# A hybrid encoder layer: both heads of a pair side by side on the array, gates and branches with stationary weights, one schedule for all heads

## What is computed

```python
h = rmsnorm(x, norm_mix)
proj = h @ w_in      # rq, rk (4 x 128), rv, rg (4 x 256), aq, ak, av (24 x 64), gates (2 x 1024)
# retention, 4 heads: q, k rotated; scores (T x T) times a decay that falls with distance both ways
ret = rms(((q @ k.T) * decay) @ v) * ret_norm
branch_a = (silu(rg) * ret) @ w_ret_out
# attention: 8 heads, each in 3 groups (window 128, dilation 1; 512, 4; 2048, 16), one softmax over
# the keys of all three
branch_b = (num / den) @ w_att_out
merged = sigmoid(gate0) * branch_a + sigmoid(gate1) * branch_b
x = x + merged @ w_out
x = x + expert_choice_ffn(rmsnorm(x, norm_ffn))   # 16 SwiGLU experts, 64 tokens of each group per expert
y = rmsnorm(x, norm_final)
```

## Time and profile before

| what | us |
|---|---|
| median of 3 runs | 2798.7 |
| profiled execution | 2800.46 |
| its span, first to last instruction | 2798.6 |
| PE busy | 2628.1 (94%) |
| DVE busy | 1607.9 (57%) |
| ACT busy | 1379.5 (49%) |
| POOL busy | 407.3 (15%) |
| mean granted TensorE clock | 0.971 |

### The profile page before, as it was taken

One profiled execution on the slowest core, in us unless ns is written; L12 is line 12 of the kernel. 1 busy time (PEld: TensorE's weight loads), 2 busy tenths in 40 slices (PEclk: granted clock), 3 DMA queues, 4 the chain that ended last, 5 costly groups with the idle time before them and its releaser, 6 DMA issues.

```text
span 2798.6 us, 42036 instructions
## 1 busy us (share of the span) xinstructions
PE 2628.1 (94%) x15186; PEld 2298.4 (82%) x15186; DVE 1607.9 (57%) x1945; ACT 1379.5 (49%) x1544; POOL 407.3 (15%) x341
## 2 busy tenths in 40 slices
PE   7999999999969999999999939999999999999995
PEld 7988888889869888888889838888888888888884
DVE  2443434432342443434432358888888888888885
ACT  4332323332243333333432227777777777777774
POOL 4121212111013212121111030000000000000000
PEclk9999999999989999999999969999999999999997
DMA  4111111112232111111122269999999999999995
GB/s 169 46 69 47 68 47 68 51 56 98 106 144 84 54 61 57 58 58 58 37 84 91 92 254 351 383 385 385 388 380 392 379 390 380 392 377 395 377 376 191
DMA packets 130053, 551.19 MB, mean 197 GB/s; under 512 B 9089, under 2 KB 9217, under 8 KB 119665
## 3 DMA queue, kind: packets, MB, share of 16 engines
q1 hardware_dynamic: 122592, 522.81, 49.0%
q0 software_dynamic: 7312, 26.39, 3.2%
HBM read 528.20 MB, written 20.97 MB: 196 GB/s over the span
## 4 chain that ended last, share of the span: by engine, by line
PE 75%; issue 17%; POOL 3%; DVE 2%; ACT 2%; DMA 1%; POOLq 0%; DVEq 0%; SPq 0%; ACTq 0%
PE bank L908 37%; PE bank L692 27%; PE bank L707 3%; PE bank L744 2%; POOL rot L539 2%; PE bank L937 2%; PE bank L771 1%; PE bank L749 1%; ACT w_hi L1001 1%; POOL w_lo L550 1%; PE bank L775 1%; PE bank L872 1%; PE bank L797 0%; DVE h_lo L1514 0%; DVE y_tile L1771 0%
## 5 line engine op out<-in xcount | busy, mean ns | idle before, releaser
L1693 DVE TENSOR_TENSOR m_lo<-m_raw,m_hi 128x2048 fp32r<-128x2048 f32 x381 | 869.9, 2291 | 123.7 <-ACT m_hi L1243 121.8
L1243 ACT ACTIVATE m_hi<-m_raw 128x2048 fp32r<-128x2048 f32 x384 | 737.3, 1921 | 266.8 <-PE bank L908 266.8
L692 PE MATMUL bank<-w_hi,h_hi 128*128 128x256 f32 (+1 forms) x2304 | 717.4, 311 | 23.1 <-issue 15.3
L692 PE MATMUL bank<-w_lo,h_hi 128*128 128x256 f32 (+1 forms) x2304 | 698.3, 303 | 0.0
L692 PE MATMUL bank<-w_hi,h_lo 128*128 128x256 f32 (+1 forms) x2304 | 698.2, 303 | 0.0
L692 PEld LDWEIGHTS bank<-w_hi,h_hi 128*128 128x128 f32 x2304 | 445.7, 193 | 35.7 <-issue 28.2
L692 PEld LDWEIGHTS bank<-w_lo,h_hi 128*128 128x128 f32 x2304 | 446.7, 194 | 0.0
L692 PEld LDWEIGHTS bank<-w_hi,h_lo 128*128 128x128 f32 x2304 | 445.7, 193 | 0.0
L908 PE MATMUL bank<-m_hi,xs_hi 128*128 128x512 f32 x1040 | 324.2, 393 | 1.4 <-DVE xs_lo L1715 1.4
L908 PE MATMUL bank<-m_hi,xs_lo 128*128 128x512 f32 x1040 | 321.2, 390 | 0.0
L908 PE MATMUL bank<-m_lo,xs_hi 128*128 128x512 f32 x1040 | 321.2, 390 | 0.0
(11 more groups left out here) (175 smaller groups left out, 3077.6 us busy)
## 6 DMA issues: line engine op xcount, KB each, us to landing
m_raw<-in_w_exp_gate SPq DMA_DIRECT2D x128, 1024.0 KB, 7.7
m_raw<-in_w_exp_up SPq DMA_DIRECT2D x128, 1024.0 KB, 7.7
m_raw<-in_w_exp_down SPq DMA_DIRECT2D x128, 1024.0 KB, 7.5
w_raw<-in_w_b SPq DMA_DIRECT2D x24, 1536.0 KB, 6.4
w_raw<-in_w_a SPq DMA_DIRECT2D x24, 1024.0 KB, 4.8
w_raw<-in_w_c SPq DMA_DIRECT2D x24, 1024.0 KB, 4.8
xt<-in_x SPq DMA_DIRECT2D x16, 512.0 KB, 6.5
w_raw<-in_w_d SPq DMA_DIRECT2D x8, 1024.0 KB, 4.8
```

The lines of the kernel that those rows point to most:

```text
L692: last = pe.matmul(ps_proj[:, proj.slot, 0:cols], a[:, c, tokens], v[:, c, :], start=c == n == 0, stop=c == chunks - 1 and n == 2)
L1243: act.activation(m_hi[slot.slot][:, :, :], m_raw[raw.slot][:, :, :], ACT.Copy)\
L1693: dve.tensor_tensor(m_lo[slot.slot][:, :, :], m_raw[raw.slot][:, :, :], m_hi[slot.slot][:, :, :].bitcast(F32), ALU.subtract)\
```

## The change

1. **Pairs.** S is split: `S r` makes the 512-column scores of both heads (a = 0, 1) for residue r, `D r` the 128-column ones, one head after the other in each group; `T r` transposes four blocks of each head, `U r` the two small ones of both; one `V` makes both heads' outputs, alternating between the heads. `prob_t` holds both heads. Each head of a pair has its bank of `ps_sc` and of `ps_out`, and PE waits for both banks.
2. **Order.** The attention units of pair 0 come first, alone. Then three times: retention head h with the scores of pair h, then the units of pair h+1, with T3, U3 and V of pair h and the *whole* retention of head h. The last head's T3, U3, V and retention lie in the first column. G comes after V. The last `R` of the attention units comes after the first tile of the next head, so no transposes end the loop's body. As the next pair's v is projected before V has read the old one, it goes to `v_next` and is copied. SP loads in the new order. The first unit is now 384 columns wide (POOL's first split 3072 elements instead of 2048).
3. **Columns.** `project_turned` takes 128 weight columns as the stationary operand and moves 512 tokens. The outputs are features by tokens, so they are what w_out needs and `merged`'s transposes go: ACT rounds the sum to `mixed_hi`, DVE takes `mixed_lo`, and w_out's first tile waits chunk by chunk (`s_mixed`). The units' order is gate 0, gate 1, branch b, branch a.
4. **Reload.** x for the residual goes to `xr`, in the place of `h_hi`, after the last gates and behind the first w_out unit; `gain_ffn` beside it. So the experts' `m_hi` slots are reversed, and ACT's second split waits until x is stored.

```diff
--- before.py
+++ after.py
...
+def head_schedule():
+    order = "P S0 P D0 P P T0 S1 P U0 D1 P P T1 S2 P U1 D2 P P T2 S3 P U2 D3 P"
+    tiles = [(u, i) for u in range(3) for i in range(NT)]
+    out, behind = [], [("R", NG - 1, NT - 1)]
+    for word in order.split():
+        if word != "P":
+            out.append((word[0], int(word[1])))
+            continue
+        u, i = tiles.pop(0)
+        out.append(("P", u, i))
+        if i < len(PIECES):
+            out.append(("W", i))
+        if behind:
+            out.append(behind.pop(0))
+        if u == 0:
+            behind.append(("R", None, i))
+    assert not tiles and not behind
+    return out
...
+def attention_schedule(tail):
+    extra = {0: (("T", 3),), 1: (("U", 3),), 2: (("V",), ("G",)), 3: (("K", 0), ("K", 1)),
+             4: (("K", 2), ("K", 3)), 5: (("O", 0), ("O", 1)), 6: (("O", 2), ("O", 3)),
+             9: (("A", 0),), 10: (("A", 1),)} if tail else {}
     out, behind = [], []
     for n in range(NG * NT):
         g, i = divmod(n, NT)
         out.append(("P", g, i))
         if i < len(PIECES):
             out.append(("W", i))
+        out.extend(extra.get(n, ()))
         if behind:
             out.append(behind.pop(0))
         behind.append(("R", g, i))
+    return out
+COLUMN_UNITS = (0, 1, 3, 2)
+FIRST_COLUMN = {(0, 0): (("T", 3),), (0, 1): (("U", 3), ("V",), ("G",)), (1, 0): (("K", 0), ("K", 1)),
+                (1, 1): (("K", 2), ("K", 3)), (3, 0): (("O", 0), ("O", 1), ("O", 2), ("O", 3)),
+                (3, 1): (("A", 0), ("A", 1))}
+def column_schedule(first):
+    out = []
+    for u in COLUMN_UNITS:
+        for cc in range(COLS):
+            out.append(("C", u, cc))
+            if first:
+                out.extend(FIRST_COLUMN.get((u, cc), ()))
     return out
...
+        def all_read(eng, frees, t, but=0):
+            done = Tally(2)
+            done.items, done.laps, done.k = t.items, t.laps, t.k - but
+            eng.wait_ge(frees[0], START + done.lap + done.slot)
+            eng.wait_ge(frees[1], START + done.lap)
...
+                    if n == 0:
+                        sp.wait_ge(s_proj, START + b * PER_BATCH["proj"] + GATES_DONE)
                         apart(sp, s_apart_sp)
                         for i in range(NT):
...
+            def project_turned(chunks, hi, lo, cc, ready=None):
+                sl = w.slot
+                wh = w_hi[sl][:, 0:chunks * NC].rearrange("p (c n) -> p c n", c=chunks)
+                wl = w_lo[sl][:, 0:chunks * NC].rearrange("p (c n) -> p c n", c=chunks)
+                pe.wait_ge(s_proj_free[proj.slot], START + proj.lap)
+                for c in range(chunks):
+                    if ready is not None and c in ready:
+                        pe.wait_ge(s_lo, ready[c])
+                    for n, (v, a) in enumerate(((wh, hi), (wl, hi), (wh, lo))):
+                        last = pe.matmul(ps_proj[:, proj.slot, :], v[:, c, natural(cc)], a[:, c, :],
...
+                elif what == "S":
+                    r = arg[0]
+                    if r == 0:
+                        all_read(pe, s_tr_free, tr, but=1)
+                    all_read(pe, s_sc_free, sc)
+                    for a in range(2):
+                        pe.matmul(ps_sc[:, a, :], qk_t[0][head_rows(a), 0, natural(r)], qk_t[0][head_rows(a), 1, :],
+                                  start=True, stop=True).then_inc(s_sc, 1)
+                        sc.k += 1
+                elif what == "D":
+                    r = arg[0]
+                    if r == 0:
+                        all_read(pe, s_tr_free, tr)
+                    all_read(pe, s_sc_free, sc)
+                    for g in (1, 2):
+                        for a in range(2):
+                            last = pe.matmul(ps_sc[:, a, P * (g - 1):P * g], qk_t[g][head_rows(a), 0, natural(r)],
+                                             qk_t[g][head_rows(a), 1, natural(r)], start=True, stop=True)
+                            if g == 2:
+                                last.then_inc(s_sc, 1)
+                                sc.k += 1
+                elif what == "T":
+                    for a in range(2):
+                        pe.wait_ge(s_prob, step.n(1))
+                        transposes([prob[a][:, natural(j)] for j in range(4)])
+                        step.k += 1
+                elif what == "U":
+                    transposes([prob[a][:, natural(j)] for a in range(2) for j in (4, 5)])
+                elif what == "V":
+                    all_read(pe, s_tr_free, tr)
+                    all_read(pe, s_out_free, outs)
+                    for r in range(RES):
+                        for a in range(2):
+                            pe.matmul(ps_out[head_rows(a), a, :], v_a[0][:, r, head_rows(a)], prob_t[:, a, r, :],
+                                      start=r == 0, stop=False)
+                    for g in (1, 2):
+                        for r in range(RES):
+                            for a in range(2):
+                                last = pe.matmul(ps_out[head_rows(a), a, natural(r)], v_a[g][:, r, head_rows(a)],
+                                                 prob_t[:, a, RES + g - 1, natural(r)],
+                                                 start=False, stop=g == 2 and r == RES - 1)
+                                if g == 2 and r == RES - 1:
+                                    last.then_inc(s_out, 1)
+                                    outs.k += 1
...
+                def column(first):
+                    los = START + b * PER_BATCH["lo"]
+                    for what, *arg in column_schedule(first):
+                        if what in "TUV":
+                            attention_step(what, arg)
+                        elif what in "KOA":
+                            retention_step(what, arg)
...
+                        elif what == "C":
+                            u, cc = arg
+                            if cc == 0:
+                                unit_ready()
+                            if u < 2:
+                                project_turned(KC, h_hi, h_lo, cc)
+                            elif u == 3:
+                                project_turned(HP, a_hi, a_lo, cc, {0: los + HP} if first else None)
                             else:
...
-                pe.wait_ge(s_merged, START + b * PER_BATCH["mix"] + 16)
-                for i in range(NT):
-                    for half in range(2):
...
+                                project_turned(KC, r_hi, r_lo, cc,
+                                               {0: los + HP + 6, 6: los + HP + 7, 7: los + HP + 8} if first else None)
+                            if cc == COLS - 1:
+                                w.k += 1
+                column(True)
+                with rolled(pe, D // NC - 1, t, PER_COL):
+                    column(False)
                 for n in range(D // NC):
                     unit_ready()
                     for i in range(NT):
-                        project(NC, KC, h_hi, h_lo, natural(i))
+                        project(NC, KC, mixed_hi, mixed_lo, natural(i),
+                                b * PER_BATCH["mix"] if n == i == 0 else None)
...
+                    outs.k += 2
+                    if tail:
+                        all_read(act, s_proj_free, proj)
+                        act.wait_ge(s_out, START + outs.n())
+                        act.activation(v_a[0][:, 0:NT - 1, :], v_next[:, :, :], ACT.Copy)
...
+                def mixed_his(first):
+                    for cc in range(COLS):
+                        act.wait_ge(s_merged, START + t["mix"].n(1))
+                        operand_hi(mixed_hi[:, bass.ds(first + cc, 1), :], gates[:, 0, cc:cc + 1, :])
+                        t["mix"].k += 1
...
+                    elif unit.k == 1:
+                        act.wait_ge(s_n2, START + NB * NT)
+                        act.wait_ge(s_store_x, 16 * NB * NT)
...
+                elif what == "D":
+                    dve.wait_ge(s_tr, tr.n())
+                    for a in range(2):
+                        dve.wait_ge(s_sc, sc.n(1))
+                        apart(dve, s_apart_dve)
+                        dve.tensor_tensor_reduce(
+                            out=prob[a][:, T:T + 2 * P], in0=ps_sc[:, sc.slot, 0:2 * P],
+                            in1=mask12[:, :], scale=1.0, scalar=-3.0e38,
+                            op0=ALU.add, op1=ALU.max, accum_out=top[:, 2 * a + 1:2 * a + 2])\
+                            .then_inc(s_sc_free[sc.slot], 1)
+                        sc.k += 1
+                        all_read(dve, s_sc_free, sc)
+                        dve.tensor_scalar(shift[:, a:a + 1], top[:, 2 * a:2 * a + 1], top[:, 2 * a + 1:2 * a + 2],
+                                          -DH ** -0.5, ALU.max, ALU.mult).then_inc(s_sm, 1)
+                        score.k += 1
+                    for a in range(2):
+                        scale_step(a)
+                elif what == "T":
...
```

(89 more changed lines are left out.)

798 lines of the change are left out of this document (341 added, 457 removed).

## The result

| | before | after |
|---|---|---|
| median | 2798.8 us | 2659.8 us (2658.7 to 2663.7, 4 runs) |
| ratio | | 0.9506 [0.9489, 0.9522] |
| profiled execution | 2800.46 us | 2658.68 us |
| its span | 2798.6 us | 2656.3 us |
| PE busy | 2628.1 us | 2498.7 us (94%) |

The forecast was 2690 us, 109 less than before; the kernel measures 139 less. The profile after, stage by stage: the end of the last column, w_out, the second group's mixer, and most of the experts (windows; columns as in the earlier trace rows).

The account below looks back on a forecast made before the run. The prediction took PE (TensorE) as the bound. Its terms summed to -55.2 us per request group, twice, plus 2 at the start: -108.4, so 2692.1 profiled and 2690 us forecast; range for 8 in 10: 2655 to 2752.

Parts of the forecast that it names:

- a, halves: In S, D and V, both heads' matmuls overlap on separate array halves, n records in n/2 + 1 slots: -31.6 us per group.
- b, stationary weights: In gates and branches, 672 matmuls of 512 columns replace 1344 of 256: -9.8 us per group.
- c, merged: Before w_out, the merged tokens' transposes and the slow start go, 1.2 us of waiting is left: -14.8 us per group.
- d, jump, with entry and exit: At the head loop's jump, queued matmuls cover part of the fetch, clock stays up: -11.8 us per group; entry and exit -2.6.
- e, small waits: Small PE waits in the heads: 7.0 us per group go, 7.2 come at D0 and behind D's scalings; net nothing.
- f, K0: Before the retention's K0, a new wait for ACT's swish, 2.8 us three times: +8.4 us per group.
- g, first column: The first column takes in the last head's T3, U3, V and retention, with new waits: +7 us per group.
- Rival 4: At the jump back: not covered, and waits e to g are twice what was counted; 2754 us, chance 0.07.
- rival 3: In S, D and V: every change of half drains the array, 312 changes, +67 us without any overlap; 2815 us, chance 0.04.

Follow-up runs that it names:

- same_half: The changed kernel with both heads of a pair using the first half of the array in S, D and V: 2737.3 us.
- after_shifted: The changed kernel with 64 unneeded transposes (128 PE instructions) ahead of everything: 2689.1 us.
- before_shifted: The kernel before with 32 unneeded transposes (64 PE instructions) ahead of everything: 2777.9 us.
- r_at_end: The changed kernel with the attention schedule's last R issued before the jump back, and S0 waiting for all transposes: 2674.2 us.
- turned_256: The changed kernel with each gate and branch tile as two runs of 256 tokens, the same weights loaded twice: 2675.8 us.

## Why the prediction was right, and where it was not

In us per request group, forecast and read from the traces:

| term | forecast | read | |
|---|---|---|---|
| a, halves | -31.6 | -41.8 | S -13.7, D -7.1, V -21.0 |
| b, stationary weights | -9.8 | -10.2 | a column's 48 matmuls 10.9 |
| c, merged | -14.8 | -14.3 | one wait of 1.66 left |
| d, jump, with entry and exit | -14.4 | -18.0 | no gap, full clock |
| e, small waits | 0 | -3.1 | 7.1 before; D0's 0.66 four times and w_lo's 0.44 three times after |
| f, K0 | +8.4 | +9.3 | 3.1 three times |
| g, first column | +7 | +4.5 | 1.10, 1.46, 1.00, 0.96 |

Twice the sum, with +1.8 once for the start, makes -145.4 us; the profiled executions differ by 141.8, so the table is true to some 4 us. It leaves out what would pull both ways: the three stretches at half clock beside K0 (5.1 us lost), two as long behind the loop's exit in before (from 544.8 and 1404.9, 3.4 us gained), and waits of before's columns for DVE's gate_s (2.8 us in all).

The prediction named 2660 us as what comes out if D overlaps fully and the jump is hidden, and that is the time measured. D did overlap; the jump was not hidden but short.

**Term a: right mechanism, wrong size.** It assumed that starts stay in order one slot apart, so that n records take n/2 + 1 slots, and took D halfway between overlap and none. They start in pairs, n/2 slots, and short records as well as long. That is 10 of the 18.4 us per group by which the terms together fell short. same_half puts the whole overlap at 77 us, where the step had 2 x (31.6 - 2.6) = 58. The rule of the Trainium skill (TensorE: Matmul & The Clock Gate, section "Part 3: Packing small matmuls") that a weight load overlaps only a matmul of another row group is not borne out: V's halves share all rows, and V takes 5.33 us for both heads where that rule, as the prediction read it, gives 10.6.

**Term d: nearly the right number, for a reason that fell.** The step said that the fetch stays and queued work covers half of it. after_shifted has that case: with 1.7 us of work left on PE, a branch of 6.1 us is bare for 4.75 and pulls the clock down, 7.3 us a jump. In after the branch takes 0.21 to 0.25 us, because the body happens to lie well. Of the 30.8 us that the four jumps gave, 23.4 came in before from 64 instructions of padding alone (before_shifted); the new place of R gives the rest, and with its other four waits some 14 (r_at_end). Had the body of after lain elsewhere, the time would have been 2689 us, the forecast, by chance. Rival 4 falls for the same reason: the jump needed no cover.

**Term c** was sized well: the last chunk of the first w_out tile waits for DVE's mixed_lo, 1.66 us against 1.2. **Term b** rests on 13 to 14 ns per matmul and holds; a wait for DVE's w_lo adds 0.44 us in three columns of each group, which I had not seen.

**Terms e and g** were charges for waits that I could not see in the trace, and both were too high: DVE had slack where I put it behind its scalings. **Term f** was read from a chain of rows and came within 1 us, 3.1 a wait against 2.8, but its last link was wrong: K0 was released by the copy of qk_t behind swish, 0.28 us after swish's end. What it left out is the clock, which the prediction named as a sign of being wrong if it fell within a head: it did so beside three of the six waits, for 5 us in all.

In the price of rival 3, 312 changes of 0.21 us are 66 us and not 67, which changes nothing.

## What to carry to other kernels

Matmuls on two halves of the array ran side by side only when they were near neighbours in the program, so interleave the heads instruction by instruction; then two cost nearly what one does. Before explaining a gap at a loop's jump by the work around it, shift the loop by some instructions: in a body of about 1700 PE instructions the place alone was worth 23 to 29 us here. A chain that is 3 us longer than its cover costs more than 3 us (28 for 18.5), in part as the clock can fall beside it: move its reader a tile later first. Before you put a wait down to another instruction than the list names, compare the distance from the end of each to the start of the waiting one over all waits and in a second kernel: the copy's was 0.34 us every time, swish's was not.

## What the runs showed of the hardware

- Halves that differ only in columns overlap as fully as halves that differ in rows: 5.33 us for 48 records in V, 10.51 when both heads use one half.
- A taken branch of PE over a body of 1692 or 1702 recorded instructions takes 0.21 to 0.25 us in four places of the body and 3.7 or 6.1 us in two others; a shift by 256 instructions gave back the short one. The jump of the loop over groups, with a body of several thousand, takes 5.9 to 6.3 us, and 7.6 in turned_256.
- After a gap of 4.75 us the granted clock was 0.50 for 4.4 us; beside six gaps of 3.1 us, with the same instructions around, a stretch at 0.50 came three times and none three times.
